# Token shift of a first projection: matmuls with shift and carry matrices, or a copy within SBUF and VectorE

## The reference

```
u = x @ w_in                                  # 256 tokens; here the first 3360 columns
z = u_r                                       # (256, 3360)
z_prev = pad(z, one zero row in front)[:-1]   # row t holds token t - 1
z = z + mu * (z_prev - z)                     # mu: one number per column
r, k, v, zw, za, zg = split(z, [1024, 1024, 1024, 64, 64, 160])
```

## Time and profile before

| | us |
|---|---|
| median of three runs | 3215.3 (3214.1 to 3218.9) |
| profiled execution, first to last instruction (span) | 3213.3 |
| TensorE busy in it | 3035.3 (94%) |
| VectorE busy | 1550.1 (48%) |
| ScalarE busy | 837.7 (26%) |
| mean granted TensorE clock, share of full | 0.971 |

### The profile page before, as it was taken

The page is one execution under the profiler, slowest core; times in us unless marked ns, Lnnn a source line. Parts: engine busy times, 40 slices in busy tenths (PEclk is TensorE's granted clock), DMA queues, the critical chain, the costliest instruction groups (busy, mean ns, idle before and its releaser), DMA issues.

```text
span 3213.3 us, 42675 instructions
## 1 busy us (share of the span) xinstructions
PE 3035.3 (94%) x18308; PEld 2171.3 (68%) x18308; DVE 1550.1 (48%) x1862; ACT 837.7 (26%) x926; POOL 266.6 (8%) x245
## 2 busy tenths in 40 slices
PE   8999999899999999999999999799999999999998
PEld 6787777899987733333333333288768878997886
DVE  4465544674555513222222322438886554444655
ACT  3342222544433311011101100110001334443443
POOL 2042111000000000000000000054330000000000
PEclk9999988999998999999999999899999999999899
DMA  7543221456564599999999999743333465887443
GB/s 243 152 136 99 74 67 55 119 161 180 177 228 152 211 413 425 425 425 425 425 425 425 425 425 425 291 140 118 117 119 118 144 175 122 184 189 158 99 158 138
DMA packets 215216, 722.10 MB, mean 225 GB/s; under 512 B 16170, under 2 KB 18634, under 8 KB 164716
## 3 DMA queue, kind: packets, MB, share of 16 engines
q1 hardware_dynamic: 210716, 702.22, 62.6%
q0 software_dynamic: 3216, 14.97, 1.3%
q10 hardware_dynamic: 1088, 2.10, 0.2%
HBM read 717.13 MB, written 2.10 MB: 224 GB/s over the span
## 4 chain that ended last, share of the span: by engine, by line
PE 73%; DMA 12%; DVE 10%; ACT 4%; issue 1%; POOL 0%; DVEq 0%; ACTq 0%
PE psum L137 72%; DMA t<-in_w_up 11%; DVE t L283 7%; ACT t L254 2%; PE psum L143 1%; DVE t L294 1%; ACT t L256 1%; DVE t L298 0%; DVE t L306 0%; ACT L254 0%; POOL t L328 0%; DVE t L269 0%; ACT L256 0%; DMA t<-in_x 0%; DVE t L275 0%
## 5 line engine op out<-in xcount | busy, mean ns | idle before, releaser
L137 PE MATMUL psum<-t,t 128*128 128x256 f32 (+10 forms) x17230 | 2941.4, 380 | 125.5 <-DVE t L283 69.3
L137 PEld LDWEIGHTS psum<-t,t 128*128 128x128 f32 (+4 forms) x17230 | 2080.0, 175 | 948.1 <-issue 580.3
L283 DVE TENSOR_TENSOR t<-t,t 128x1024 fp32r<-128x1024 f32 (+6 forms) x642 | 785.0, 1223 | 502.1 <-ACT t L254 469.1
L254 ACT ACTIVATE t<-t 128x1024 fp32r<-128x1024 f32 (+8 forms) x521 | 528.5, 1014 | 924.5 <-PE psum L137 661.2
L283 DVE TENSOR_TENSOR t<-t,psum 128x1024 f32<-128x1024 f32 (+3 forms) x265 | 246.4, 930 | 739.5 <-PE psum L137 439.0
L254 ACT ACTIVATE t<-psum 128x1024 f32<-128x1024 f32 (+5 forms) x278 | 213.5, 768 | 1408.7 <-PE psum L137 1310.4
L328 POOL TENSOR_TENSOR t<-t,t 128x1024 f32<-128x1024 f32 (+9 forms) x125 | 209.0, 1672 | 545.4 <-DVE t L283 258.2
L283 DVE TENSOR_TENSOR t<-psum,t 128x1024 f32<-128x1024 f32 (+5 forms) x125 | 100.2, 802 | 131.6 <-PE psum L137 103.0
L143 PE MATMUL psum<-t,t 128*128 128x128 f32 (+1 forms) x566 | 87.7, 294 | 32.1 <-DVE t L294 18.4
L143 PEld LDWEIGHTS psum<-t,t 128*128 128x128 f32 (+1 forms) x566 | 67.3, 149 | 69.6 <-issue 39.8
L83 POOL DMA_DIRECT2D t<-in_s_lr x1 | 0.6, 574 | 1185.1 <-DVE t L306 1185.1
(11 more groups left out here) (65 smaller groups left out, 237.9 us busy)
## 6 DMA issues: line engine op xcount, KB each, us to landing
t<-in_w_gate SPq DMA_DIRECT2D x128, 1024.0 KB, 16.9
t<-in_w_up SPq DMA_DIRECT2D x128, 1024.0 KB, 18.4
t<-in_w_down SPq DMA_DIRECT2D x128, 1024.0 KB, 17.4
t<-in_w_in SPq DMA_DIRECT2D x160, 512.0 KB, 4.3
t<-in_w_in_odd SPq DMA_DIRECT2D x128, 512.0 KB, 5.3
t<-in_w_in_even SPq DMA_DIRECT2D x96, 512.0 KB, 3.8
t<-in_w_out SPq DMA_DIRECT2D x32, 512.0 KB, 4.7
t<-in_w_pg SPq DMA_DIRECT2D x32, 512.0 KB, 4.1
```

Source lines behind the costliest of these rows:

```text
L137: ins = self.e.matmul(o, l, r, start=start, stop=stop, skip_group_check=True)
L254: self.put(self.e.activation(o, i, f, scale=scale), event)
L283: self.put(self.e.tensor_tensor(o, a, b, op), event)
```

## The change

The shift and carry matrices go, with their matmuls, their PSUM bank and Pool's five instructions. In their place ScalarE, after copying a chunk to `UR`, waits for its copy and for VectorE's end of the chunk two before, and issues two DMAs within SBUF: partitions 0 to 126 of `UR` to partitions 1 to 127 of a buffer, both halves, and token 127 into row 0 of the buffer's second half. There are two buffers, `earlier`, used in turn; row 0 of the first half is the zero row. VectorE splits up to piece 8 ci + 12, waits for the landing, subtracts, multiplies by mu and adds (all in SBUF), and clears row 0 of the first half again. TensorE goes from chunk to chunk without a wait of its own and waits for the constants after the last.

```diff
@@ build
-        ident, shiftd, carry, ucent, tri_inc, tri_str = [alloc(128) for _ in range(6)]
+        ident, diag0, diag1, ucent, tri_inc, tri_str = [alloc(128) for _ in range(6)]
...
+        earlier = [at(o, 1024).rearrange("p (b c) -> p b c", b=2) for o in (fmbase + 3360, lt_at + 2304)]
...
-        diag = [shiftd, carry]
+        diag = [diag0, diag1]
@@ tensor_program
+            for ci in range(1, 7):
+                proj_a(pe, f"ur{ci}", xT, 16, "w_in", 512 * ci, min(512, 3360 - 512 * ci))
             pe.wait_ge(("consts",))
-            for ci, c in enumerate(range(0, 3360, 512)):
-                n = min(512, 3360 - c)
-                if ci:
-                    proj_a(pe, f"ur{ci}", xT, 16, "w_in", c, n)
-                v = half(pe.take("ur.shift", ci))[:, :, 0:n]
-                d = UR[:, :, 512 * ci:512 * ci + n]
-                pe.wait_ge(("ur.copied", ci))
-                pe.mm(v[:, 0, :], shiftd, d[:, 0, :], True, True)
-                pe.mm(v[:, 1, :], shiftd, d[:, 1, :], True, False)
-                pe.mm(v[:, 1, :], carry, d[:, 0, :], False, True, event=("ur.shift", ci))
@@ vector_program
-            v.stage("in")
+            for z in earlier:
+                v.mset(z[0:1, 0, :], 0.0, event=("ur.first",))
...
             for ci, c in enumerate(range(0, 3360, 512)):
                 n = min(512, 3360 - c)
-                v.ahead_of("ur.shift", ci)
-                ps = half(v.bank("ur.shift", ci))[:, :, 0:n]
-                d = UR[:, :, 512 * ci:512 * ci + n]
-                v.wait_ge(("ur.shift", ci), ("landed.mu",))
-                v.tt(ps, ps, two(mub[:, 512 * ci:512 * ci + n], n), ALU.mult)
-                v.tt(d, d, ps, ALU.add, event=("ur", ci))
-                v.free("ur.shift", ci)
+                v.split_to(8 * ci + 12)
+                d, z = UR[:, :, c:c + n], earlier[ci % 2][:, :, 0:n]
+                v.wait_ge((f"landed.shift{ci % 2}", ci), ("landed.mu",))
+                v.tt(z, z, d, ALU.subtract)
+                v.tt(z, z, two(mub[:, c:c + n], n), ALU.mult)
+                v.tt(d, d, z, ALU.add, event=("ur", ci))
+                v.mset(z[0:1, 0, :], 0.0)
@@ scalar_program
-                out_of(f"ur{ci}", UR[:, :, c:c + n], 0, event=("ur.copied", ci))
+                d, z = UR[:, :, c:c + n], earlier[ci % 2][:, :, 0:n]
+                out_of(f"ur{ci}", d, 0, event=("ur.copied", ci))
+                a.wait_ge(("ur.copied", ci), ("ur", ci - 2) if ci > 1 else ("ur.first",))
+                a.load((f"landed.shift{ci % 2}", ci), [(z[1:128], d[0:127]), (z[0:1, 1], d[127:128, 0])])
@@ pool_program
-            g.memset(shiftd, 0.0)
-            g.asel(shiftd, shiftd, ALU.not_equal, 1.0, 1, [[-1, 128]], 1)
-            g.asel(shiftd, shiftd, ALU.not_equal, -1.0, 0, [[-1, 128]], 1)
-            g.memset(carry, 0.0)
-            g.asel(carry, carry, ALU.not_equal, 1.0, -127, [[128, 128]], 1)
```

## The result

The changed kernel takes 3362.6 us (median of four runs, 3359.2 to 3367.6) against 3217.1 for the kernel before, also over four runs: ratio 1.0454, 95% interval 1.0436 to 1.0472. That is 145.5 us more; 3361 was predicted, in a range of 3310 to 3425. Its median was 3217.1 to 3222.2 us from one time to the next, so a difference between two runs that were measured at different times is good to a few us.

What follows compares the result with a forecast made beforehand. TensorE, busy 94% of the span, was taken as the bound. Five longer periods (+104.8), chunk 6 (+24.9) and the tail (+16) make +145.7 us on 3215.3, giving 3361, range 3310 to 3425.

Steps and rivals of the forecast that it cites:

- D decides everything: D is the copy's time from issue to landing; the period equals the old 26.3 us at D = 8.15.
- One engine, equal shares: Engines get equal row shares, so prime 127 rows put all 254 packets on one engine; 90% for one engine.
- D = 26.6: Copy of 512 columns, issue to landing: 22.6 us on one engine plus 4.0 for weight packets in between.
- A period of 47.25: Each of five periods between copies of chunks 0 to 5: 44.75 us plus 2.5, 20.95 more than before.
- the clock's price: TensorE at a lower clock after idling: taken as 2.5 us per period.
- The last chunk 42.1: Chunk 6, with 288 columns, takes 42.1 us against 17.25 before: +24.9.
- The tail +16: After chunk 6, up to the low-rank matmuls: VectorE's result 16.5 us later, less 1.6 slack, plus 1 for the clock.
- E + 5.6: Time, counted from the end E of a chunk's matmuls, at which TensorE needs the piece from ScalarE's next split.
- one gap of 22 us: TensorE idles some 22 us in each chunk, waiting for VectorE's split while VectorE waits for the DMA.
- one packet more: ScalarE's second DMA issue per chunk, moving a single row, was counted as one packet more.
- Rival 1: Sixteen engines share the copy, landing in 4.3 us at most, period 22.4: 3196 us, faster; 8%.

Runs made afterwards that it cites:

- Two forms of Pool's copy: Changed kernel with Pool issuing 112, 15 and 1 rows: 3217.7 us; the same with VectorE's one-row fill ahead of the wait, clearing the other buffer: 3215.4 us.

## Why the prediction was right, point by point

- **D decides everything**: shown. Only the cut of the rows was changed, the landing went from 27.1 us to 16.2, 11.4 and 4.6, and the time from 3362.6 to 3290.5, 3262.3 and 3218.2. The same edits shorten ScalarE's issues too; Pool's copy of 127 rows, with ScalarE free and the time no better, takes that rival away. Below D of some 5 us other costs decide.
- **One engine, equal shares**: shown by the packets, by 27 GB/s and by the runs with 122, 96 and 112 rows. The argument behind it, that no row showed an unequal share, was weaker than its outcome: Pool's queue does share unequally. It held because the copy is on ScalarE's queue: there 127 rows took one engine in both forms (landing in 27.1 us, and 27 GB/s), while on Pool's queue they took one in the first (30.1 us) and several in the other (3.1 us, up to 18 packets at once). The 16 completions that the forecast gives a store are in the trace: the first of the four stores has 16 packets of 4 bytes from 3207.73 to 3207.87 us, and 16 landing events from 3208.09 to 3208.22.
- **D = 26.6**: 27.1 in the chunk shown, 25.6 to 27.3 over the six wide ones. The 254 packets take 23.3 to 25.2 us from the first to the end of the last, 1.9 to 3.9 more than 254 x 0.084 = 21.3; 4.0 was forecast for the weights' packets between them. **A period of 47.25**: 46.9 on average (234.5 / 5). The waits add up as said, and the clock's price too: after the gap four pieces took 13.0 to 14.2 us where 11.2 + 2.5 was forecast. The 2.5 was the author's estimate, and no run shows that figure itself: in its place they show 1.8 to 3.0 us more for the four pieces, with the granted clock at 0.50 from 72.1 to 74 us, 0.81 up to 78 and 1.00 from there on.
- **The last chunk 42.1**: 42.5.
- **The tail +16**: from the copy of chunk 6 to the low-rank matmuls 34.35 us, 15.8 more than before. Here the number is right by luck, and the path is wrong. The forecast has TensorE wait for VectorE's fill. In the trace it waits for the gates, which ScalarE computes after VectorE's last result, and from there it works without a break up to the low-rank matmuls:

```profile
338.01 0.31 ACT L254 ACTIVATE t<-t 128x128 f32<-128x128 f32 x1 [7.39 <-DVE t L283]
...
340.25 1.89 PE L143 MATMUL psum<-t,t 128*64 128x128 f32 x8 [4.50 <-ACT t L254]
```

  The same matmuls in the kernel before:

```profile
199.03 1.06 PE L143 MATMUL psum<-t,t 128*64 128x128 f32 x8 [0.54 <-ACT t L254]
```

  VectorE's result came 18.8 us later than before, not 16.5: the landing took 17.8, and the three narrow operations 4.3 us instead of 2.5, since one ran beside Pool. Of the 18.8, 5.3 were slack, because in the kernel before ScalarE came to the gates only at 196.88, that long after the result at 191.53. And 2.3 came on top: from 340.25 to 349.5 the granted clock was 0.73, and these matmuls and the two pieces behind them took 9.3 us instead of 7.0. 18.8 - 5.3 + 2.3 is 15.8. VectorE's fill ended 1.6 us before TensorE came to the low-rank matmuls in both kernels, so it held nothing up, and the 1.6 us that the forecast took off as slack stayed as they were.
- **What the forecast missed**: that ScalarE can't split while its issue is held. It let the next split come later by two short issues, in time for TensorE at E + 5.6. It predicted one gap of 22 us on TensorE; there are two, 11.3 and 7.4, with two pieces at the lower clock between them:

```profile
56.40:64.70 8.30, 8.29 (x24) 6.30 (x24) 1.22 (x1) 2.10 (x2) 0.00 (x0) 0.67 0.44 141
72.10:85.15 13.05, 13.01 (x49) 10.52 (x50) 6.12 (x5) 3.18 (x3) 0.00 (x0) 0.87 0.64 202
```

  The granted clock was 0.67 while the two pieces between the gaps took 8.3 us instead of 5.6, and 0.87 over the four after the second gap, after standing for 7.4 us. The first gap and its slow pieces cost nothing, since the landing ends later.
- The single row was not "one packet more" but 16 pieces. The pieces take only 0.011 us each, but its issue is the one that stood for 12.5 to 14.5 us.
- **Rival 1** (16 engines) was priced at 3196. With the copy cut for 16 and 15 engines the kernel takes 3218: the price left out that ScalarE's splits wait for its issues, and that VectorE's operations beside Pool's take 2.7 to 2.9 us in the tail, not 0.77. Even without any copy it is 3204.

In the profile, 143.5 of the span's 147.6 us more arise before the low-rank matmuls. The remaining 4.1 lie behind them and weren't followed; that is about the scatter of the runs.

## What to carry to other kernels

Before a matmul is replaced by a copy, write down the copy's row count and who issues it: 127 rows, a prime number, ran on one engine from ScalarE's queue, and cutting them into 112 and 15 brought 27.1 us down to 4.6. Count as costs of the copy also the time its issue holds the issuing engine, and where else its consumer's operands now lie: beside Pool, two operands in SBUF were nearly four times as dear as one in PSUM (2.88 us against 0.77). And first move the work that waits: placing the same matmuls one piece later gave 6 us for a few lines.

## What the runs showed that was not expected

- An issue can hold ScalarE for long: the two of a wide chunk took 13.3 to 15.3 us together when one engine had the long copy, three took 4.9 to 5.3 with two engines and 2.4 to 2.9 with 16, and a store at the end of the kernel 0.38. The long copy's own issue is short (0.7 to 1.4 us); one behind it stands (12.5 to 14.5). What holds it isn't shown: the single row wasn't issued first in any run.
- The same copy of 127 rows by two halves lands 3 us later from Pool's queue than from ScalarE's, and its data start 3.5 us later. Cut into two copies of 127 rows, each lands in 3.1 us from Pool.
- TensorE came back at the lower clock after gaps of 5.8, 7.4 and 24.7 us alike: four pieces then took 14.1, 13.0 and, after the longest, 13.3, at granted clocks of 0.79, 0.87 and 0.85.
- Two forms of Pool's copy (3217.7 and 3215.4) show no clear gain in time, though the low-rank matmuls start 2.1 and 5.8 us earlier in their profiles. The second profile is of the fastest of eleven runs, 12 us under their median, so it flatters that form. Why the rest is lost stays open; the scatter of the runs is as large.
